# Two transformer blocks in fp32 on one core: seven products for one more weight pair per turn of the second FFN, with squares and residual adds moved between engines

## The reference, cut to what matters

```
h2 = rms_norm(x, g_ff)                                  # 256 x 2048
x  = x + square(relu(h2 @ w_ff1)) @ w_ff2               # w_ff1 2048 x 8192, w_ff2 8192 x 2048
```

## Time and profile before

| | |
|---|---|
| time, median of 3 runs | 2575.62 us (2575.19 to 2575.97) |
| span of the profiled execution | 2573.7 us; some 1.9 us of a run lie outside of it |
| busy: PE, DVE, ACT, POOL | 100%, 78%, 56%, 21% |
| busy: weight loads of PE | 83% |
| granted TensorE clock | 1.000 (2.4 GHz) all through |
| second FFN | from about 1910 us to the end |
| DMA in the second FFN | 66 to 69% busy, about 215 GB/s |

### The profile page before, as it was taken

The page is one execution under the profiler, slowest core; times in us unless marked ns, Lnnn a source line. Parts: engine busy times, 40 slices in busy tenths (PEclk is TensorE's granted clock), DMA queues, the critical chain, the costliest instruction groups (busy, mean ns, idle before and its releaser), DMA issues.

```text
span 2573.7 us, 34186 instructions
## 1 busy us (share of the span) xinstructions
PE 2567.3 (100%) x11501; PEld 2134.4 (83%) x11501; DVE 2015.8 (78%) x2102; ACT 1451.4 (56%) x1615; POOL 536.5 (21%) x1034
## 2 busy tenths in 40 slices
PE   9999999999999999999999999999999999999999
PEld 8888888888888888888878888888888888888888
DVE  6767888666988888888886655566679988998895
ACT  5546666445565555555555557774455555555553
POOL 2212221233112112222133120003322112211121
DMA  8666666766688888888787655556666766666674
GB/s 274 210 206 212 216 197 208 255 214 209 209 238 246 245 241 244 247 242 243 240 291 216 210 183 195 174 191 211 223 202 215 231 206 218 201 220 206 206 228 154
DMA packets 291153, 564.76 MB, mean 219 GB/s; under 512 B 28512, under 2 KB 41872, under 8 KB 290544
## 3 DMA queue, kind: packets, MB, share of 16 engines
q1 hardware_dynamic: 247616, 502.25, 59.0%
q0 software_dynamic: 43264, 61.18, 10.5%
q10 hardware_dynamic: 176, 0.07, 0.0%
HBM read 503.75 MB, written 2.10 MB: 197 GB/s over the span
## 4 chain that ended last, share of the span: by engine, by line
PE 97%; DVE 1%; DMA 1%; SPq 0%; DVEq 0%; ACT 0%; issue 0%; ACTq 0%
PE pair L2491 22%; PE pair L2486 22%; PE pair L2495 22%; PE pair L2776 8%; PE aux L2776 6%; PE aux L2761 3%; PE aux L2755 3%; PE aux L2758 3%; PE pair L2758 1%; PE pair L2755 1%; PE pair L2761 1%; PE aux L2653 0%; DMA raw<-in_w_ffn_down 0%; PE aux L2648 0%; PE pair L2573 0%; PE pair L2566 0%
## 5 line engine op out<-in xcount | busy, mean ns | idle before, releaser
L845 ACT ACTIVATE w_hi<-raw 128x1024 fp32r<-128x1024 f32 (+1 forms) x786 | 818.2, 1053 | 722.1 <-PE pair L2495 571.4
L1499 DVE TENSOR_TENSOR w_lo<-raw,w_hi 128x1024 fp32r<-128x1024 f32 (+1 forms) x788 | 937.7, 1214 | 342.1 <-ACT w_hi L845 323.2
L2486 PE MATMUL pair<-w_hi,lhs_hi 128*128 128x512 f32 x1568 | 422.6, 391 | 0.8 <-ACT lhs_hi L897 0.8
L2491 PE MATMUL pair<-w_hi,lhs_lo 128*128 128x512 f32 x1568 | 419.7, 389 | 0.6 <-DVE lhs_lo L1552 0.5
L2495 PE MATMUL pair<-w_lo,lhs_hi 128*128 128x512 f32 x1568 | 419.7, 389 | 0.0
L766 POOL DMA_DIRECT2D arena<-arena x528 | 262.4, 603 | 668.9 <-DVE arena L2003 291.0
L2491 PEld LDWEIGHTS pair<-w_hi,lhs_lo 128*128 128x128 f32 x1568 | 294.2, 188 | 63.0 <-DVE lhs_lo L1552 1.4
L2495 PEld LDWEIGHTS pair<-w_lo,lhs_hi 128*128 128x128 f32 x1568 | 294.0, 188 | 62.2 <-DVE w_lo L1499 1.0
L2486 PEld LDWEIGHTS pair<-w_hi,lhs_hi 128*128 128x128 f32 x1568 | 292.2, 188 | 60.6 <-ACT lhs_hi L897 1.2
L2486 PE MATMUL pair<-w_hi,low_hi 128*128 128x512 f32 (+1 forms) x992 | 263.4, 387 | 0.0
L2491 PE MATMUL pair<-w_hi,low_lo 128*128 128x512 f32 (+1 forms) x992 | 262.0, 386 | 0.0
(11 more groups left out here) (366 smaller groups left out, 3244.1 us busy)
## 6 DMA issues: line engine op xcount, KB each, us to landing
raw<-in_w_ff SPq DMA_DIRECT2D x128, 1024.0 KB, 5.2
raw<-in_w_in SPq DMA_DIRECT2D x118, 1024.0 KB, 5.3
raw<-in_w_ffn_down SPq DMA_DIRECT2D x44, 1024.0 KB, 5.1
raw<-in_w_ffn_gate SPq DMA_DIRECT2D x80, 512.0 KB, 6.6
raw<-in_w_ffn_up SPq DMA_DIRECT2D x80, 512.0 KB, 7.5
raw<-in_w_out SPq DMA_DIRECT2D x32, 1024.0 KB, 5.7
arena<-arena POOLq DMA_DIRECT2D x840, 32.0 KB, 4.4
xres<-sums POOLq DMA_DIRECT2D x36, 512.0 KB, 9.8
```

Of the source, the lines that this page charges most:

```text
L845: nc.scalar.activation(w_hi[:, at.slot(p, k), :, 0:width], raw[:, at.raw_slot(p, k), 2 * h:2 * h + 2, 0:width], ACT.Copy).then_inc(hi_read ...
L1499: v.tensor_tensor(w_lo[:, at.slot(p, k), :, 0:n], raw[:, at.raw_slot(p, k), 2 * h:2 * h + 2, 0:n], w_hi[:, at.slot(p, k), :, 0:n].bitcast( ...
L2486: nc.tensor.matmul(ps[:, t, 0:n], hi_t[:, ch, tok], w_hi[:, s, c, 0:n], start=start and k == 0 and c == 0, stop=False)
L2491: nc.tensor.matmul(ps[:, t, 0:n], lo_t[:, ch, tok], w_hi[:, s, c, 0:n], start=False, stop=False)
```

## The change

```diff
-FIVE = (0, 1, 3, 5, 7)
+FIVE = (1, 3, 4, 6, 7)          # turn 0 (before: SEVEN, units 1 3 5 7)
+SIX = (0, 1, 3, 4, 6, 7)        # turns 1 to 6 (before: FIVE, units 0 1 3 5 7)
+MAIN = {SEVEN: SEVEN, FIVE: FIVE[1:], SIX: FIVE[1:]}

 # POOL
-            with pool.Fori(NB1 + T_FF2, NB1 + NB2 + T_FF2) as b:
-                move(b)
+            def add_part(j, i):
+                pool.wait_ge(sums_copied, i * 3 + (COPIES1 + j + 1))
+                pool.sem_inc(moving, 1)
+                pool.dma_start(xres[:, :, j * N:(j + 1) * N], gates, accum_op=ALU.add).then_inc(parts_added, 16)
+            move(NB1 + T_FF2)
+            with pool.Fori(0, TURNS2 - 1) as i:
+                for n in range(2):
+                    move(i * 2 + (NB1 + T_FF2 + 1 + n))
+                for j in range(3):
+                    add_part(j, i)
+            for n in range(2):
+                move(NB1 + T_FF2 + 2 * TURNS2 - 1 + n)
+            add_part(0, TURNS2 - 1)
+            move(NB1 + T_FF2 + 2 * TURNS2 + 1)
+            add_part(1, TURNS2 - 1)
+            add_part(2, TURNS2 - 1)

 # ACT
+            def relu_squares(rows):
+                for t in range(TOK):
+                    nc.scalar.activation(rows[:, t, :], rows[:, t, :], ACT.Relu, scale=x_inv[:, t:t + 1])
+                act.drain()
+                nc.scalar.activation(rows, rows, ACT.Square)
+                act.drain().then_inc(act_ready, 1)
+            def copy_part(at, j, i):
+                panel_done(at, 2 + j)
+                if j == 0:
+                    act.wait_ge(flipped, i * 2 + (NB1 + T_FF2 + 3))
+                if j > 0 or not isinstance(i, int) or i > 0:
+                    act.wait_ge(parts_added, i * 48 + 16 * j)
+                nc.scalar.activation(gates, pairs[at.pair(2 + j)][:], ACT.Copy).then_inc(sums_copied, 1)
             def block2(at, i, last=False, units=SIX):
+                act.wait_ge(gran_used, at.gran(0) + SPLIT)
+                hid_turn(b, 0, T_FF2 - 1)
+                hi_ordinary(at, 2, None)
+                hi_sums(3, n, units)
+                hi_seven(at, 3, None)
+                hi_seven(at, 4, None)
+                hi_sums(4, n, units)
+                hi_ordinary(at, 5, None)
+                hid_turn(b + 1, 4, T_FF2 - 1)
+                for u in (6, 7):
+                    hi_seven(at, u, None)
+                    hi_sums(u, n, units)
...
+                relu_squares(gates)
                 hi(at, 3, 0, 1)
+                relu_squares(hid)
                 hi(at, 3, 1, 4)
+                copy_part(at, 0, i)
...
                 hi(at, 4, 0, 4)
                 if last:
                     hid_turn(b + 2, 0, T_FF2 - 1, dst=last_hi)
+                copy_part(at, 1, i)
                 hi(at, 5, 0, 4)
                 if last:
+                    copy_part(at, 2, i)
                     hi(at, 6, 0, 2)
                     hid_turn(b + 3, 4, T_FF2 - 1, dst=last_hi)
                     hi(at, 6, 2, 4)
                 else:
                     nxt = At("ffn2", i + 1)
+                    hi_sums(0, n + 1, SIX)
+                    copy_part(at, 2, i)
+                    hi_seven(nxt, 0, None)
+                    hi_sums(1, n + 1, SIX)
+                    hi_seven(nxt, 1, None)

 # DVE, before turn 0: pair_forms(2, one_pair, one_sum) and one_lo for unit 1; in turn 0 zero_* take the place of first_*
 # DVE
             def block2(at, i, last=False, units=SIX):
-                unit_pair(at, 2, n, False, five)
                 hid_turn(b)
-                unit_pair(at, 4, n, False, five)
-                unit_pair(at, 6, n, False, five)
+                sums_seven(at, 3, n, units)
+                lo_ordinary(at, 2)
+                lo_sums(3, n, units)
+                lo_blocks(at, 3)
+                sums_seven(at, 4, n, units)
+                lo_blocks(at, 4)
+                lo_sums(4, n, units)
+                lo_ordinary(at, 5)
+                for u in (6, 7):
+                    sums_seven(at, u, n, units)
+                    lo_blocks(at, u)
+                    lo_sums(u, n, units)
                 hid_turn(b + 1, 4)
                 lo(at, 2, 0, 2)
-                recombine(at, n, 0, five)
+                if units == SIX:
+                    dve.wait_ge(parts_added, i * 48)
+                recombine(at, n, 3, units)
                 lo(at, 2, 2, 4)
                 dve.wait_ge(act_ready, b + 3)
-                (the squaring multiplies, both blocks, L2418 and L2425)
                 flip(b + (2 + T_FF2), ..., n_split=1)
...
-                add_x(at, 2, 0)
-                add_x(at, 3, N)
-                add_x(at, 4, 2 * N)
 # DVE after turn 6
+            dve.wait_ge(parts_added, TURNS2 * 48)

 # PE, seven(): order of the products, and the waits
                 product(aux[:, 0, :], tokens(0, c), block_of(B12), True)
                 product(q0[:, 0, :], tokens(0, c + 1), block_of(B22), fresh)
-                (T2 with its wait for both halves of the low sums, then B21, gran_used, T1, T3, T4)
+                product(aux[:, 3, :], form(S4), block_of(B21), fresh).then_inc(gran_used, 2)
+                (wait for the first half of the low sums, then T1, T3, wait for the second, T2, T4;
+                 in the last unit of a turn T2 comes before T1)
 # PE, block2(): gemm of P4 waits for the copy of part 0, P5 for part 1, the next turn (P6 after turn 6) for part 2
+                bank_free(at, 2)
+                for g in range(2):
+                    pe.wait_ge(moved_taken, i * 2 + (NB1 + T_FF2 + 1 + g))
+                    gemm(at, 2, low, groups=[g])
+                gemm(at, 3, low)
+                for j in range(2, 4):
+                    gemm(at, 2 + j, low, free=copied(i * 3 + (COPIES1 + j - 1)))
```

More of the change, by code:

```diff
@@ L476, in up_loads, with sevens, buffer_of @@
         return i * 32 + (u // 4 * 16 + 16)
[L478 to L490, removed]
+    def sevens(i, u, units):
+        n = units.index(u)
+        if units == SEVEN:
+            return i * len(SEVEN) + n
+        if units == FIVE:
+            return TURNS1 * len(SEVEN) + n
+        return i * len(SIX) + (n + TURNS1 * len(SEVEN) + len(FIVE) - (TURNS1 + 1) * len(SIX))
+    def buffer_of(u, units):
+        b = (units.index(u) + (units == SIX)) % 2
+        return t_sum[b], t_his[0 if units == SEVEN else b], t_lo[b]
     def two_slots(ring, at, p, k):
@@ L2379, in _ @@
             lo(at, 1, 4, 6)
+            pair_forms(2, one_pair, one_sum)
             dve.wait_ge(s_hi_ready, 2)
@@ L2430, in block2 @@
-                if not five:
-                    first_forms()
-                lo(at, 4, 0, 4)
-                add_x(at, 3, N)
+                flip(b + (2 + T_FF2), by_chunk(gates), n_split=1)
+                lo(at, 3, 0, 4)
+                if units == FIVE:
+                    pair_forms(0, zero_pair, zero_sum)
+                lo(at, 4, 0, 4)
+                dve.wait_ge(act_ready, b + 4)
                 flip(b + (3 + T_FF2), by_chunk(hid), n_split=1)
@@ L2458, in block2 @@
                     lo_blocks(nxt, 1)
-                    lo_sums(1, n + 1, True)
-            block2(At("ffn2", 0), 0, five=False)
+                    lo_sums(1, n + 1, SIX)
+            block2(At("ffn2", 0), 0, units=FIVE)
             with dve.Fori(1, TURNS2 - 1) as i:
@@ L2742, in _, with ordinary @@
             gemm(at, 1, wide)
-            def ordinary(at, u, five=False):
+            def ordinary(at, u, units=SEVEN):
                 p, k0 = unit(u)
@@ L2761, in ordinary, with seven, product @@
                         mm = nc.tensor.matmul(bank[t, w], lhs_hi[:, ch, tok], w_lo[:, s, w, :], start=False,
-                                              stop=u == 6 and c == 1 and (t, w) == (1, 0))
+                                              stop=u == (6 if units == SEVEN else 5) and c == 1 and (t, w) == (1, 0))
                     mm.then_inc(gran_used, 1)
-            def seven(at, u, i, five=False):
+            def seven(at, u, i, units=SEVEN):
                 p, k = unit(u)
                 q0, q1 = pairs[at.pair(0)], pairs[at.pair(1)]
-                n = order(five).index(u)
                 b_hi, b_lo = two_slots(w_hi, at, p, k), two_slots(w_lo, at, p, k)
-                first, last, c = n == 0, n == len(order(five)) - 1, 2 * u
-                def product(bank, s_pair, t_pair, fresh):
+                first, last, c = u == units[0], u == units[-1], 2 * u
+                fresh = units == SIX
+                def product(bank, s_pair, t_pair, begins):
                     for s, t, a, z in ((s_pair[0], t_pair[0], True, False), (s_pair[1], t_pair[0], False, False),
                                        (s_pair[0], t_pair[1], False, True)):
-                        mm = nc.tensor.matmul(bank, s, t, start=fresh and first and a, stop=last and z)
+                        mm = nc.tensor.matmul(bank, s, t, start=begins and first and a, stop=last and z)
                     return mm
@@ L2790, in sum_of, with second @@
                 def sum_of(f):
```

(5 more changed lines are left out.)

229 lines of the change are left out of this document (109 added, 120 removed).

## The result

The changed kernel takes 2620.8 us (median of 4 runs, 2619.9 to 2621.6) against 2575.8 us beside it on the same chip: ratio 1.0174, 95% interval 1.0160 to 1.0189. It is 45 us slower. Forecast was 2614.7, with 2606 to 2622 as the forecast's own range.

The account below looks back on a forecast made before the run. PE was taken as the bound with DVE close behind. To 2575.6 us it added 6.7 (turn 0), 5 x 4.05 (turns 1 to 5), 4.05 and 8.1 (turn 6), together 39.1: 2614.7 us, range 2594 to 2627, the forecast's own 2606 to 2622.

Parts of the forecast that it names:

- The price of a seven: Unit phase: a unit by seven products takes DVE 7.02 us against 2.27 for an ordinary one, 4.75 us more.
- the restarts: Steady turn: PE stalls and restarts before unit 3 (1.5 us), unit 7 (1.3 us) and P2 (2.1 us).
- The panel phase costs nothing more: Panel phase of steady turns: ACT's added work and part 0's landing are hidden, 0 us, with +1.5 kept for the range.
- Rival C: Accumulating DMAs set every turn, ACT waiting 2 us longer in each: 2629 us, chance 0.10.
- The extra cost of the seven: Turns 1 to 6: DVE's added unit-phase work makes each 4.05 us longer, saved product counted.
- Turn 0: First turn of the second FFN: more DVE work before the recombining starts P2 6.7 us later, bounds 2 and 8.
- The last turn: Turn 6: P6 waits for the last move, part 1's DMA and ACT's copy, starting 8.1 us later.
- The clock: Behind the pause before P6: idle PE may fall to 1.2 GHz, a few us more, not put in the sum.
- Rival A: DVE keeps up because its whole load per turn falls, so PE keeps its pace: 2569.0 us, chance 0.09.

Follow-up runs that it names:

- e2: Changed kernel with two low parts per turn written twice on DVE: unit 5's in the unit phase, 2638.9 us; panel 4's in the panel phase, 2620.9 us.
- e4: Changed kernel with DVE's first add of the recombining moved ahead of the first two low parts of panel 2: 2620.3 us.
- e7: Changed kernel with both edits, e3's (DVE adds panels 2 to 4) and e4's (first add moved ahead): 2597.7 us.
- e1: Changed kernel with low parts of units 4, 5 and 6 written for only 8 of 512 columns in turns 1 to 6: 2605.4 us.
- e3: Changed kernel with DVE adding the residual of panels 2 to 4 again, without ACT copies or accumulating DMAs: 2611.7 us.
- e11: Changed kernel with only the sixth pair undone, unit 4 ordinary again in every turn: 2617.3 us.
- e6: Changed kernel with the low parts of the transposed activations subtracted on POOL instead of DVE: 2635.0 us.
- e10: e9 with the last two low parts of panel 2 made before the last four adds of the recombining: 2615.9 us.
- e9: Changed kernel, six pairs kept: DVE adds panels 2 to 4, only panel 5 by accumulating DMA, some low parts earlier, first add ahead: 2598.3 us.
- e12: e11 plus the edits of e3 and e4, with unit 3's low blocks ahead of its low sums: 2592.8 us.

## Why the prediction was right, and where it wasn't

**The price of a seven and the restarts.** Here E, the end of the last matmul's pace in the turn before, is 2209.01, and DVE starts at E + 1.85 as before. `lo_blocks`(3) was forecast at E + 14.5 to 16.3 and ran at 14.5 to 16.2; the first add at E + 42.95, measured 42.87; P2 at E + 44.5, measured 44.45. Stalls of 1.5, 1.3 and 2.1 came out as 1.33, 1.36 and 2.18, counted from start to start with a pace of 0.23 in them. A list that runs without a gap can be added up to a tenth of a us. e2 shows that the time hangs on this list.

**What the forecast had and didn't see.** "The panel phase costs nothing more" was true to half a us in most turns, and by a chain that came out as told (part 0 issued at E + 61.1 and landed at E + 71.5, forecast 72). But it leaves no slack: the loop through POOL and the DMA closes at the same 88 us (e4, e7). Rival C's loop is shorter than the turn by 0 to 1 us only. Once it showed: in turn 1's panel phase part 0 took 11.3 us to land, ACT waited 5.0 us instead of 3.9, the next unit 0 stood 1.2 us for its low parts, and from P2 to P2 it took 88.8. The extra cost of the seven as the one cause of 4.05 us was right as a sum and incomplete as a cause: the turn's 4 us stand on three legs, DVE's whole list, the tail behind the slots of units 4 and 5, and the loop. Taking one leg away gives 0 to 2.6 us (e1, e3, e4, e11).

**Turn 0.** 6.7 forecast, 6.7 measured, and by the list as told: with the 2.3 us below taken off, the add of `pair` 0 starts at 1984.7 (forecast 1984.9) and P2 at 1986.2 (forecast 1986.2). On TensorE it shows as pauses of 2.5, 0.9 and 1.9 us beyond the pace, before unit 1, unit 7 and P2, 1.6 us of low clock, 0.5 in small steps, less the 0.7 of the product saved. The low clock is not a cost of its own here: in e3 it didn't fall in this turn, a pause of 1.3 us before unit 3 stands in its place, and P2 (1987.31, that kernel being 1.1 us late at the start) is 6.7 us behind the kernel before as well. Beside these, all of the changed kernel ran 2.3 us late before the second FFN, in code that didn't change; the other kernels of this study have 0.8 to 2.2 of it. What causes it stays open.

**The last turn.** 8.1 forecast, 7.6 measured, by the queue as told: DVE's last `hid_turn`, POOL's 16 moves, part 1's DMA behind them, ACT's copy. The landing took 9.8 us (2554.75 to the copy at 2564.59), not 10.9. e3 takes the DMAs away and P6 follows at once.

**The clock.** This is the term that was left out. It fell in three places, behind pauses of 2.75 us (1946.16 to 1948.91), 2.2 us (2339.35 to 2341.58) and 7.7 us (2562.43 to 2570.15), each time to 1.2 GHz for the next 7 to 9 matmuls, 0.427 us each against 0.2267: 1.6, 1.6 and 1.9 us. The first is hidden behind DVE's list (turn 0, above), so 3.5 us of the 6.1 by which the sum was short are clock. The rest is the 2.3 us before the second FFN and turn 1's late landing, 0.75, less the 0.5 of the last turn. It fell in turn 4 and not in the six other turns, where the pause before P2 was 2.1 to 2.2 us as well. Turn 4's P2, against turn 3's 1.19 us for four matmuls above:

```profile
2341.58 1.81 PE L2536 MATMUL pair<-w_hi,low_hi 128*128 128x512 f32 x4 [1.84 <-DVEq L2102]
```

The forecast cited the Trainium skill ("TensorE: Matmul & The Clock Gate", Part 1), by which an idle TensorE falls back to 1.2 GHz. The trace agrees behind P6's pause (granted clock 0.50) and the other two, but not behind those six.

**Rival A** (load counts, not order) is out: DVE's busy time fell by 2 us a turn and the turn grew by 4.

## What to carry to other kernels

When an engine works end to end in one phase and waits in the next, price a change by its list in that phase, item by item; the sum over the loop says nothing. Then look for the bounds that lie right behind the first: the path from the last ring slot set free to the next stage, and every loop that closes over a turn through a queue and a DMA. If two of them are of one length, single edits look worthless (e3 in the turns, e4), and only both together show what they are worth (e7). Compare turns at one clock, too: 1.6 us of low clock can look like a gain or a loss of the edit. And ask what the change saves at best before it is made: here 4.8 us of 2575, for 4.75 us more of DVE in each phase that had 2.6 to spare.

## What the runs showed of the hardware that I had not expected

- A subtraction of 128x1024 on POOL (2.4 to 3.3 us) holds up DVE's subtractions beside it: 4.57 us for two instead of 2.35, so DVE lost 2.2 us beside 2.5 to 3.1 us of POOL's work (e6).
- The granted clock can fall behind pauses of 2.2 to 3.2 us, and the length of the pause doesn't tell whether it does. It fell at unit 0 in five of six turns of e4 (pauses of 2.5 to 3.2 us; the sixth is 1.8), and at P3 in six of seven turns of e10 (2.6 us each). The same pause of 2.75 us ahead of unit 1 of turn 0 stands in eleven other kernels besides the changed one: in e3, e4, e9 and e12 the pace stayed behind it, in the changed kernel and the other seven it fell. What decides it stays open.
- Low clock isn't always lost time. In e4 eight matmuls at 0.427 us made unit 0 1.6 us longer, but TensorE still had to wait for DVE before unit 7 (0.83 us from start to start), so by this trace P2 came no later for it.
- The accumulating DMAs of 512 KB landed 9.2 to 11.3 us after their issue where 16 moves stood ahead of them, and 5.3 to 8.8 us where none did, against 5.9 to 13.0 in FFN 1. In turn 3 ACT's copy could start 10.4 us after the issue (2270.14 to 2280.53).
